# Layer one's feed-forward features as seven block products in place of eight, in groups of four

## The reference

```python
mod = jax.nn.silu(c) @ w_mod[l] + b_mod[l]
sh1, sc1, gt1, sh2, sc2, gt2 = jnp.split(mod[:, None, :], 6, axis=-1)
...
x = x + gt2 * swiglu(modulate(rms_norm(x, g_norm2[l]), sh2, sc2), w_ffn_in[l], w_ffn_out[l])

def swiglu(h, w_in, w_out):
    g, u = jnp.split(h @ w_in, 2, axis=-1)
    return (jax.nn.silu(g) * u) @ w_out
```

## Time and profile before

| | |
|---|---|
| median of the runs | 2358.67 us (2358.09 to 2359.34) |
| span of the profiled execution | 2353.3 us, 5.4 us less than the median run |
| TensorE busy | 2282.4 us (97%) |
| VectorE, ScalarE, GpSimd busy | 1358.8, 1015.9, 855.5 us |
| mean granted TensorE clock | 0.995 of full speed |

### The profile page before, as it was taken

How to read it: one execution, slowest core, us unless ns; L and a number is a source line. 1 busy time by engine, 2 the same in 40 slices (tenths; PEclk the granted TensorE clock), 3 DMA queues, 4 the chain that set the end, 5 groups by cost and what they waited for, 6 DMA issues and landing times.

```text
span 2353.3 us, 32869 instructions
## 1 busy us (share of the span) xinstructions
PE 2282.4 (97%) x12848; PEld 2069.8 (88%) x12848; DVE 1358.8 (58%) x2069; ACT 1015.9 (43%) x1992; POOL 855.5 (36%) x594
## 2 busy tenths in 40 slices
PE   6999999999999989999999999999999999999999
PEld 5888899999999989999999997788878877888887
DVE  6666677799967754654342446668879844111111
ACT  5666666642253242212212237666763354322222
POOL 2666212100034424443343336752220254544443
PEclk9999999999999999999999999999999999999999
DMA  7101111032224424443433331111113232333333
GB/s 271 38 28 37 37 37 40 25 112 77 72 81 156 145 71 131 121 126 112 138 118 119 102 97 55 37 46 46 45 35 110 94 111 91 108 99 99 97 94 96
DMA packets 134809, 208.96 MB, mean 89 GB/s; under 512 B 12544, under 2 KB 66048, under 8 KB 134400
## 3 DMA queue, kind: packets, MB, share of 16 engines
q1 hardware_dynamic: 134656, 206.86, 27.9%
HBM read 202.62 MB, written 4.19 MB: 88 GB/s over the span
## 4 chain that ended last, share of the span: by engine, by line
PE 80%; DVE 11%; ACT 5%; issue 2%; DMA 1%; POOL 1%; SPq 1%; DVEq 0%; ACTq 0%
PE acc L726 21%; PE acc L728 20%; PE acc L727 20%; DVE X L1874 4%; PE sco L927 3%; PE aux L728 3%; PE aux L727 3%; PE aux L726 3%; PE aux L940 3%; ACT M L1199 2%; PE acc L962 1%; DVE M L1740 1%; PE aux L905 1%; DVE WLO L1740 1%; DVE NM L1786 1%
## 5 line engine op out<-in xcount | busy, mean ns | idle before, releaser
L618 POOL TENSOR_TENSOR WLO<-STG,WHI 128x512 fp32r<-128x512 f32 (+2 forms) x500 | 689.7, 1401 | 1390.1 <-ACT WHI L1195 1223.8
L726 PE MATMUL acc<-H,WHI 128*128 128x384 f32 (+2 forms) x1976 | 711.6, 360 | 16.7 <-DVE H L2040 8.6
L728 PE MATMUL acc<-H,WLO 128*128 128x384 f32 (+2 forms) x1976 | 693.7, 351 | 0.0
L727 PE MATMUL acc<-H,WHI 128*128 128x384 f32 (+2 forms) x1976 | 693.5, 351 | 0.0
L1195 ACT ACTIVATE WHI<-STG 128x512 fp32r<-128x512 f32 (+2 forms) x616 | 330.2, 585 | 396.1 <-PE acc L728 357.8
L726 PEld LDWEIGHTS acc<-H,WHI 128*128 128x128 f32 x1976 | 373.1, 189 | 49.7 <-issue 17.5
L727 PEld LDWEIGHTS acc<-H,WHI 128*128 128x128 f32 x1976 | 373.2, 189 | 24.7 <-issue 0.2
L728 PEld LDWEIGHTS acc<-H,WLO 128*128 128x128 f32 x1976 | 372.6, 189 | 25.2
L726 PE MATMUL acc<-RB,WHI 128*128 128x384 f32 (+1 forms) x816 | 288.6, 354 | 3.2 <-DVE RB L1740 1.4
L1740 DVE TENSOR_TENSOR T<-G,acc 128x384 f32<-128x384 f32 (+1 forms) x101 | 60.3, 597 | 394.5 <-PE acc L728 294.6
L728 PE MATMUL acc<-RB,WLO 128*128 128x384 f32 (+1 forms) x816 | 287.6, 352 | 0.0
(11 more groups left out here) (163 smaller groups left out, 2808.6 us busy)
## 6 DMA issues: line engine op xcount, KB each, us to landing
STG<-in_w_fi SPq DMA_DIRECT2D x176, 256.0 KB, 2.7
M<-in_w_mod SPq DMA_DIRECT2D x56, 512.0 KB, 4.6
STG<-in_w_in SPq DMA_DIRECT2D x104, 256.0 KB, 2.7
STG<-in_w_gate SPq DMA_DIRECT2D x96, 256.0 KB, 2.7
STG<-in_w_fo SPq DMA_DIRECT2D x64, 256.0 KB, 2.7
STG<-in_w_br SPq DMA_DIRECT2D x96, 128.0 KB, 2.1
FIRST<-in_w_mod SPq DMA_DIRECT2D x8, 1024.0 KB, 15.7
SOONB<-in_w_mod SPq DMA_DIRECT2D x16, 512.0 KB, 3.7
```

The lines of the kernel that those rows point to most:

```text
L618: nc.gpsimd.tensor_tensor(WLO[:, s, a:a + w], STG[:, g, a:a + w], WHI[:, s, a:a + w].bitcast(F32), ALU.subtract).then_inc(S("w_split"), 1)
L726: nc.tensor.matmul(dst, lh, rh, start=first, stop=False)
L727: nc.tensor.matmul(dst, lh, rl, start=False, stop=False)
L728: return nc.tensor.matmul(dst, ll, rh, start=False, stop=last)
```

## The change

Layer one's features from the fifth on are no longer a gate and an up product each. The gate and up rows of a feature's weights and the two halves of the 1024 inputs make a 2 by 2 block matrix, the inputs' halves and the two halves of the tokens another, and their product is made with seven block products of 4 chunks by 384 tokens in place of eight (Winograd's form of Strassen's algorithm). `GROUPS` becomes six groups (4, 4, 4, 4, 4 and 2 features); the first group stays plain. The sums of blocks that this needs are `T1` to `T4` of the inputs, made once, and `S1` to `S4` of the weights, for every feature. The products lie in the four halves of `sco`; ScalarE and VectorE combine them. Of the seven low parts of the weights VectorE makes three (`VECTOR_LOWS`) and GpSimd four. A feature's weights come as four loads (`pair_load`). The pieces of `w_mod` have two slots in place of four and are spread over the features and down tiles anew. All seven of their vectors are turned by transposes now. Layer two's own feed-forward part keeps its groups.

```diff
-GROUPS = [(0, 8), (8, 8), (16, 6)]
+GROUPS = [[(0, 4), (4, 4), (8, 4), (12, 4), (16, 4), (20, 2)], [(0, 8), (8, 8), (16, 6)]]
 SLOTS, STAGES = 3, 2
+OPS = ("A11", "S3", "A12", "S1", "S2", "A22", "S4")
+OPERANDS = ("B11", "T3", "B21", "T1", "T2", "T4", "B22")
+ROLES = "acadbcd"
+VECTOR_LOWS = (0, 1, 3)
...
-RAW_UP = [[0, 2, 2, 2, 2, 2, 2, 2], [2] * 8, [2] * 6]
-RAW_DOWN = [[1] * 8, [1] * 6 + [0, 0], [0] * 8]
-TURN_UP = {(0, 6): 0, (1, 2): 2}
-TURN_DOWN = {(0, 4): 1, (2, 2): 6}
-TURNED = [0, 1, 2, 6, 3, 4, 5]
-RAW_SLOTS = 4
+RAW_UP = [0, 6, 3, 0]
+RAW_DOWN = [[2] + [1] * 5 + [0, 0], [1] * 6 + [0, 0], [1, 1, 0, 2, 2, 2, 0, 0], [2] * 6 + [0, 0], [2] * 6 + [0, 0], [2] + [0] * 7]
+TURN_DOWN = {(0, 7): 1, (2, 3): 2, (3, 2): 3, (4, 1): 4, (4, 4): 5, (5, 3): 6}
+TURNED_BEFORE = [0, 1, 2, 3, 3, 4, 5]
+RAW_SLOTS = 2
...
-        RAW = [M[:, D * i:D * (i + 1)] for i in range(RAW_SLOTS)]
+        def RAW(i):
+            if i % RAW_SLOTS == 0:
+                return M[:, 0:D]
+            return K[:, K_COS:K_COS + D] if i < KC else M[:, 3 * D:4 * D]
...
+        def raws_upto(group, kind, i):
+            places = [v[:2] for v in raw_steps() if v[1][0] == group]
+            at_ = places.index((kind, (group, i))) + 1 - RAW_LAG // (2 if kind == "up" else 1)
+            if (kind, i) == ("down", KC - 1):
+                at_ = len(places)
+            if at_ <= 0:
+                return 0
+            return raws(0, places[at_ - 1][0], group, places[at_ - 1][1][1]).stop
...
-                if i < RAW_SLOTS:
-                    sp.wait_ge(S("h_ready"), 2 * KC)
-                else:
+                if i == 0:
+                    sp.wait_ge(S("t_ready"), 2)
+                if i >= RAW_SLOTS:
                     sp.wait_ge(S("gv"), 2 * (i - RAW_SLOTS + 1))
+                if i == KC + 1:
+                    sp.wait_ge(S("t_ready"), 4)
...
-                for g, (k0, n) in enumerate(GROUPS):
-                    for f in range(n):
+                for g, (k0, n) in enumerate(GROUPS[l]):
+                    for f in range(plain(l, g)):
                         for s in range(2):
                             tile(w_fi[l, f * 2 + (2 * k0 + s)], KC * P)
-                            if l == 0:
-                                raws_behind(c.at("tile") - first_tile)
+                        if l == 0:
+                            raws_behind(g, "up", f)
+                    pairs, after = pairs_of(l, g), pairs_of(l, g + 1)
+                    for p in pairs[2:]:
+                        pair_load(p)
+                    c.step("tile", 7 * len(pairs) // 2)
                     for j in range(KC):
+                        if j < STAGES and pairs:
+                            lows_made(pairs[-2])
+                        if j == 4 and after:
+                            pair_load(after[1])
                         tile(w_fo[l, j][:, k0 * P:(k0 + n) * P], n * P)
                         if l == 0:
-                            raws_behind(c.at("tile") - first_tile)
+                            raws_behind(g, "down", j)
+                    if after:
+                        pair_load(after[0])
...
+            def feature_pair(p):
+                l, g, f, x = pair_list[p]
+                w = HALF
+                for i in range(7):
+                    if i == 0 and p:
+                        pe.wait_ge(S("mix_read"), mix_read(p - 1, "g"))
+                    elif i == 1 and p:
+                        pe.wait_ge(S("mix_made"), mix_made(p - 1, "c21"))
+                    elif i == 2:
+                        pe.wait_ge(S("mix_read"), mix_read(p, "y"))
+                    elif i == 3 and p:
+                        pe.wait_ge(S("mix_made"), mix_made(p - 1, "c12"))
+                    elif i == 4 and p:
+                        pe.wait_ge(S("mix_made"), mix_made(p - 1, "u"))
+                    elif i == 5:
+                        pe.wait_ge(S("mix_read"), mix_read(p, "z"))
+                    elif i == 6:
+                        pe.wait_ge(S("mix_made"), mix_made(p, "v"))
+                    name = OPERANDS[i]
+                    if p == pairs_of(l, g)[0] and i in (0, 1, 3, 4):
+                        pe.wait_ge(S("col_sum"), 1 + sum(v < (g, 0) for v in TURN_DOWN))
+                    if p == first_pair[l] and name in BLOCK_SUMS:
+                        pe.wait_ge(S("t_ready"), BLOCK_SUMS.index(name) + 1)
+                    low, value = low_ready(p, i)
+                    pe.wait_ge(S(low), value)
+                    hi_, lo_ = half_slot(WHI, x + i), half_slot(WLO, x + i)
+                    first = i in (0, 1, 3, 4)
+                    for k in range(4):
+                        mm = product(BANK[ROLES[i]][:, 0:w], hi_[:, k * P:(k + 1) * P], lo_[:, k * P:(k + 1) * P],
+                                     operand(name, 0)[:, k, :], operand(name, 1)[:, k, :], first and k == 0, k == 3, not first)
+                    mm.then_inc(S("mix_full"), 1)
...
+            def hi_half():
+                x = split.at("half")
+                t, h = divmod(x, 2)
+                if x >= 2 * SLOTS:
+                    name, value = half_end[x - 2 * SLOTS]
+                    if h == 0 or (name, value) != half_end[x - 2 * SLOTS - 1]:
+                        act.wait_ge(S(name), value)
+                if tile_width[t]:
+                    s, i = t % SLOTS, load_no[t]
+                    a, w = halves(tile_width[t])[h]
+                    act.wait_ge(S(f"w_load{i % STAGES}_{h}"), i // STAGES * 16 + 16)
+                    nc.scalar.activation(WHI[:, s, a:a + w], STG[:, i % STAGES, a:a + w], ACT.Copy).then_inc(S("w_hi"), 1)
+                else:
+                    p, i = pair_halves[x]
+                    name = OPS[i]
+                    if name in ADDED:
+                        act.wait_ge(S("s_add"), 4 * p + ADDED[name])
+                    else:
+                        act.wait_ge(S(f"pair{turn_of(p)}"), 64 * (loaded_before(p) + 1))
+                    nc.scalar.activation(half_slot(WHI, x), pair_store(p, RAW_PLACE[name]), ACT.Copy).then_inc(S("w_hi"), 1)
+                split.step("half")
...
+            def feature_pairs_out(ps):
+                for p in ps:
+                    l, _, _, x = pair_list[p]
+                    w = HALF
+                    for i in range(7):
+                        if i == 0 and p > ps[0]:
+                            second_silu(p - 1)
+                        act.wait_ge(S("mix_full"), 7 * p + i + 1)
+                        if i == 0:
+                            if p:
+                                act.wait_ge(S("mix_made"), mix_made(p - 1, "c12"))
+                            fn(mix("Y"), BANK["a"][:, 0:w], ACT.Copy, sem="mix_read")
+                        elif i == 1:
+                            if p > first_pair[l]:
+                                act.wait_ge(S("mix_made"), mix_made(p - 1, "b"))
+                            fn(mix("Z"), BANK["c"][:, 0:w], ACT.Copy, sem="mix_read")
+                            if p > ps[0]:
+                                mid_half_hi(p - 1, 1)
+                        elif i == 2:
+                            if p > first_pair[l]:
+                                act.wait_ge(S("mix_made"), mix_made(p - 1, "m0"))
+                            fn(mix("G"), BANK["a"][:, 0:w], ACT.Silu, sem="mix_read")
+                        hi_half()
+                    mid_half_hi(p, 0)
+                if ps:
+                    second_silu(ps[-1])
+                    mid_half_hi(ps[-1], 1)
...
+            def block_sums(l, *names):
+                if names[0] == "T1":
+                    for a, w, st in norm_parts(TOK):
+                        own("t_add", nc.vector.tensor_scalar(MM[:, 0, a:a + w], MM[:, 0, a:a + w], MOD[:, l, SH2, 0, st:st + 1], None, ALU.add))
+                for name in names:
+                    a, b = {"T1": ("B12", "B11"), "T3": ("B22", "B12"), "T2": ("B22", "T1"), "T4": ("B21", "T2")}[name]
+                    own("t_add", tt(block_sum(name), block_sum(a), block_sum(b), ALU.subtract))
+            def block_lows(*names):
+                for name in names:
+                    dve.wait_ge(S("t_hi"), BLOCK_SUMS.index(name) + 1)
+                    tt(operand(name, 1), block_sum(name), operand(name, 0).bitcast(F32), ALU.subtract).then_inc(S("t_ready"), 1)
...
+            def feature_pairs_out(ps):
+                for p in ps:
+                    l, g, _, _ = pair_list[p]
+                    w = HALF
+                    q = p + 1 if p < ps[-1] else None
+                    bank = lambda v: BANK[v][:, 0:w]
+                    done = lambda i: dve.wait_ge(S("mix_full"), 7 * p + i + 1)
+                    if q:
+                        weight_sum(q, "S1")
+                        weight_sum(q, "S3")
+                    if p > ps[0]:
+                        second_product(p - 1)
+                    if q:
+                        weight_sum(q, "S2")
+                    if p > ps[0]:
```

(55 more changed lines are left out.)

354 lines of the change are left out of this document (242 added, 112 removed).

## The result

The changed kernel takes 2421.97 us (2419.58 to 2423.89), the kernel before 2358.38 (2357.79 to 2359.34) in the same rounds: ratio 1.0269, 95% interval 1.0255 to 1.0284. It is slower by 63.6 us. I had forecast 2393 and a range up to 2412: the sign was right, the loss nearly twice the one worked out, the time outside the range.

What follows compares the result with a forecast made beforehand. TensorE, busy 97% of the span, was taken as the bound. Work saved (-34.7 us) plus waits and slow clock summed to +34.5 on 2353.3, so 2387.8; the runs' median lies 5.4 higher: 2393 us, range 2358 to 2412.

Steps and rivals of the forecast that it cites:

- The products: In 18 features, one product of 12 matmuls less each, at 0.1733 us a matmul: 37.4 us saved.
- The waits: New TensorE waits, by place: second feature 1.3, third 9.4, first down tiles 7.5, product features 11, other down groups 30.8, last 7.5.
- The third feature: Its first silu, behind `hi` for a late weight tile, ends at 893.2 where TensorE wanted 883.8: +9.4, bounds 7 and 12.
- The features: In 13 seven-product features the third product starts late behind ScalarE's copy, 0.85 us each: +11, bounds 0 and 20.
- first down group: Down tiles after the plain features: pieces wait for the low part of `T4`, residuals come late: +7.5, bounds 4 and 10.
- last: Last down group: tiles of 2.08 us, but VectorE needs about 27 us against 18: +7.5, bounds 4 and 11.
- The clock, +1.7: After the third feature's wait, the granted clock stands at 0.50 for some 4 us: +1.7, nothing if it holds.
- a step with two single pieces: In later down groups, a weighing of 1.5 and a load of 4.0 plus 0.1: 5.6 us against 4.16.
- the weight sums at the sixth tile: In down groups, the piece and three weight sums (3 x 0.61) on VectorE hold the residual by 2 us.
- Feeding stays hidden: Rival, 10%: loads land before needed and ScalarE's copies run early; -23 us, 2336.
- Slots are no bound: Rival, 16%: loads of about 3 us serve steps of 4.2; 38 us of waits, +3, 2362.
- The lock on the chain: Rival, 13%: GpSimd's split blocks VectorE just before `S1`'s low part or `S4` in 13 features, 1.29 us more each; +17, 2410.

## Why the prediction missed

*The products, -37.4.* Right. 84 matmuls in 14.56 us were measured when nothing disturbed a feature. At full-speed distances the matmuls and transposes of the part take 503.6 us for 539.5 before, 36 less; the forecast had 34.7 less.

*The waits.* The steps of the sum, without transposes and clock, came to 67.5 us of waits. TensorE's idle time in the part rose by 61.1. To it comes some 0.26 us for each of the 47 waits, 12 us in all: a wait is counted from the end of the last matmul, 0.16 us past the point where the next would have started, and the first distance behind it is 0.10 longer. That makes 73 for 67.5. The places were those named, and the sizes are mostly close. The third feature: 10.7 for 9.4, behind the `hi` that was named. The features: 15.27 us each in place of 15.41 (9.5 came back with the low part moved, forecast 11). Part of that difference is a reading of mine: the silu at 862.18 in the earlier trace rows stands directly behind the `hi` copy of 861.14, so that its 0.42 us are not TensorE's delay alone; the next one, at 866.18, comes 0.26 us behind the first matmul of the next product. Measured by stage length against the sum (in brackets), slow clock included: first down group 45.3 (42.6), second 40.7 (36.6), third 46.0 (41), fourth 52.4 (44.7), fifth 52.2 (46.1), last 28.4 (26.4). All six are over, most of all the two with twelve pieces each.

*The clock, +1.7.* This is the term that failed. I priced the slow clock once, after the longest hole, and there 1.7 us were lost by the start times. Every wait of 1 to 5 us in the down tiles I priced as if TensorE went on at full speed behind it. The drop in the earlier trace rows stands behind a pause of 4.4 us, not behind one of the length of my hole, and waits of that size were in my own sum. PE's row of the kernel before:

```profile
837.68 0.66 PE L726 MATMUL acc<-H,WHI 128*128 128x384 f32 x1 [4.36 <-DVE H L2040]
```

In the changed kernel a pause of 1.8 us stands ahead of such a drop too. Measured over the part are 20 us for my 1.7. The stretch grew by 60.3 us, 25.8 more than forecast. In TensorE's time that is 18.6 more for the slow clock, 5.5 more for the waits with their restarts, 1.2 less for the products, and some 3 in other longer distances.

This divides TensorE's time, not the causes. In the down tiles VectorE and DMA often set the pace, and a matmul that had been faster would have waited instead: the transposes took 5.4 us of slow matmuls out of two stages and gave back 3.3. So the steps of those stages were mis-sized as well. I had 5.6 us for a step with two single pieces; 8.9 and 6.3 were measured (1248.14 to 1257.05 and 1268.72 to 1275.00), the first with a vector's closing reduction of 1.4 us in it and with the clock at 1.00 until TensorE's wait began, with loads of 4.5 us in the median and up to 6.1 where I took 4.0. How much of the 25.8 us each of the two would have cost alone, no run shows.

*Two things more in the down groups.* I had the weight sums at the sixth tile as work of 2 us, not as a wait for the last load in the queue; residual to residual is 9.9 us there. And I took loads of 4.0 us in steps that carry a piece, a down tile and a feature's blocks at once: in the fourth group's down tiles DMA moved 368 GB/s in one window of 4 us at a share of 1.03, and the waits for pieces there are up to 2.2 us. More slots alone gave back 20 us.

*The rivals.* Feeding stays hidden: wrong. Slots are no bound: wrong, by 20 us. The lock on the chain: seen on low parts and weighings, but the feature was shorter than forecast, not longer by 1.3, so it is not what made up the 29 us.

*Outside the part.* Of the 3 us ahead of it, 2.4 stand there after the first 31 us of the program, and between the traces of the changed kernel and its variants the same matmul ahead of the part moves from 838.3 to 841.1: as far as these runs show they are spread, not a cost of the change. The 3 behind lie at the start of layer two, 10.8 us from the last residual to its first product where there were 8.1; no run here isolates them.

## What to carry to other kernels

When TensorE is the bound, price each wait of a few us twice: the pause, and the matmuls behind it at half the clock; where another engine then sets the pace, the second part is an upper bound. When work of the bounding engine is removed or its stages cut finer, ask where the work beside it will stand: here 36 us of saved matmuls needed a new place for 56 loads and weighings, and found it mostly in the idle gaps of VectorE within the new features, not in the down tiles. Move the feed first, then count the saving.

## What the runs showed of the hardware

- A pause of 4.2 us, 1253.6 to 1257.7, was followed by a window at 0.50, and so was one of 1.8 us, 1161.9 to 1163.7. At the lower level matmuls of 384 columns start 0.32 us apart, at the full one 0.173. In product features, with waits of 0.3 us each, the clock stayed at 1.00 over 60 us.
- Idle pauses filled with transposes whose result nobody reads raised the granted clock of a stage from 0.87 to 0.97, and the program with 144 more instructions was not slower (ratio 1.0244 for 1.0269).
- A wait of TensorE cost some 0.26 us more than its idle time, 47 times in the part.
- Block sums over 1536 columns took 1.76 us each, as scaled from narrower operations, but their low parts 1.76, 2.86 and 2.85, while four of GpSimd's low parts beside them took 9.06 us where four alone would take 5.2.
